# The up projection of a squared-ReLU MLP as seven products of halves, with its weights streaming

## The reference, cut to what matters

```python
h = rmsnorm(x, mix_norm)
b_gate, c_gate, v = jnp.split(h @ w_in, 3, axis=-1)      # (512 x 2048) @ (2048 x 6144)
y = (b_gate * causal_conv3(c_gate * v)) @ w_out          # (512 x 2048) @ (2048 x 2048)
x = x + y
g = rmsnorm(x, mlp_norm)
a = relu(g @ mlp_w1)                                     # (512 x 2048) @ (2048 x 8192)
x = x + (a * a) @ mlp_w2                                 # (512 x 8192) @ (8192 x 2048)
```

## Time and profile before

| | us |
|---|---|
| median of 3 runs (2037.37 to 2037.85) | 2037.64 |
| the profiled execution, whole | 2034.88 |
| its span, first to last instruction | 2033.1 |
| TensorE busy in it | 2015.3 (99%) |
| VectorE busy in it | 1217.7 (60%) |
| ScalarE busy in it | 657.8 (32%) |

### The profile page before, as it was taken

The page is one execution under the profiler, slowest core; times in us unless marked ns, Lnnn a source line. Parts: engine busy times, 40 slices in busy tenths (PEclk is TensorE's granted clock), DMA queues, the critical chain, the costliest instruction groups (busy, mean ns, idle before and its releaser), DMA issues.

```text
span 2033.1 us, 22629 instructions
## 1 busy us (share of the span) xinstructions
PE 2015.3 (99%) x8900; PEld 1665.6 (82%) x8900; DVE 1217.7 (60%) x1362; ACT 657.8 (32%) x876; POOL 30.6 (2%) x62
## 2 busy tenths in 40 slices
PE   8999999999999999999999999999999999999999
PEld 7888888888888888787888888888888888888887
DVE  6345353353543453535364554636988989978878
ACT  6222222222233332323232232323444443333432
POOL 0000000000000000000000000000000000000000
PEclk9999999999999999999999999999999999999999
DMA  5322223222223222536263553639899888888783
GB/s 187 114 93 103 95 91 104 97 88 103 83 104 103 100 87 104 196 118 229 99 248 128 204 198 138 244 108 364 321 359 353 314 336 316 320 316 322 272 316 139
DMA packets 72965, 387.10 MB, mean 190 GB/s; under 512 B 7984, under 2 KB 7984, under 8 KB 41264
## 3 DMA queue, kind: packets, MB, share of 16 engines
q1 hardware_dynamic: 64672, 327.18, 44.3%
q0 software_dynamic: 8064, 58.72, 6.9%
q10 hardware_dynamic: 144, 0.04, 0.0%
HBM read 323.00 MB, written 62.91 MB: 190 GB/s over the span
## 4 chain that ended last, share of the span: by engine, by line
PE 99%; issue 0%; DMA 0%; ACT 0%; DVE 0%; ACTq 0%
PE pair L682 68%; PE pair L781 30%; PE pair L748 0%; DMA cols<-in_cols 0%; PE pair L712 0%; PE pair L705 0%; PE pair L715 0%; PE pair L718 0%; ACT L284 0%; DVE x L601 0%; ACT h_hi L284 0%; ACT w_hi L280 0%; ACTq L340 0%
## 5 line engine op out<-in xcount | busy, mean ns | idle before, releaser
L391 DVE TENSOR_TENSOR w_lo<-w_raw,w_hi 128x512 fp32r<-128x512 f32 x512 | 352.3, 692 | 677.2 <-ACT w_hi L280 671.9
L682 PE MATMUL pair<-h_hi,w_lo 128*128 128x512 f32 x1788 | 698.5, 391 | 6.9 <-issue 6.9
L682 PE MATMUL pair<-h_hi,w_hi 128*128 128x512 f32 x1788 | 695.9, 389 | 0.0
L682 PE MATMUL pair<-h_lo,w_hi 128*128 128x512 f32 x1788 | 695.6, 389 | 0.0
L280 ACT ACTIVATE w_hi<-w_raw 128x512 fp32r<-128x512 f32 x512 | 323.0, 631 | 951.6 <-PE pair L682 949.1
L781 PE MATMUL pair<-d_w,act_hi 128*128 128x512 f32 x1792 | 551.6, 389 | 0.0
L682 PEld LDWEIGHTS pair<-h_hi,w_lo 128*128 128x128 f32 x1788 | 335.6, 188 | 78.2 <-issue 9.5
L781 PEld LDWEIGHTS pair<-d_w,act_hi 128*128 128x128 f32 x1792 | 336.3, 188 | 69.9 <-issue 0.2
L682 PEld LDWEIGHTS pair<-h_hi,w_hi 128*128 128x128 f32 x1788 | 335.6, 188 | 70.2
L682 PEld LDWEIGHTS pair<-h_lo,w_hi 128*128 128x128 f32 x1788 | 335.7, 188 | 69.7 <-issue 0.5
L333 ACT ACTIVATE d_w<-d_raw 128x1024 fp32r<-128x1024 f32 x224 | 233.7, 1059 | 369.6 <-PE pair L781 235.3
(11 more groups left out here) (55 smaller groups left out, 571.9 us busy)
## 6 DMA issues: line engine op xcount, KB each, us to landing
w_raw<-in_weights SPq DMA_DIRECT2D x127, 1024.0 KB, 4.9
d_raw<-in_down SPq DMA_DIRECT2D x64, 1024.0 KB, 8.5
spill<-stage POOLq DMA_DIRECT2D x56, 1024.0 KB, 6.0
act_hi<-spill SPq DMA_DIRECT2D x112, 512.0 KB, 6.5
act_lo<-spill SPq DMA_DIRECT2D x112, 512.0 KB, 7.3
resid<-in_xt SPq DMA_DIRECT2D x3, 1024.0 KB, 12.9
out<-x SPq DMA_DIRECT2D x6, 512.0 KB, 3.3
resid<-in_xt SPq DMA_DIRECT2D x4, 256.0 KB, 6.0
```

Source lines behind the costliest of these rows:

```text
L391: nc.vector.tensor_tensor(w_lo[:, k % RING, :], w_raw[:, k // GRAN % NRAW, k % GRAN, :], w_hi[:, k % RING, :].bitcast(F32), ALU.subtract). ...
L682: mm = nc.tensor.matmul(ps[NT * parity + i], stationary, moving, start=(k == 0 and j == 0), stop=(k == KT - 1 and j == 2))
```

## The change

The up projection is done in the same seven-product way. The 16 up blocks go; 16 more turns stand ahead of the 16 of the down projection, numbered `v` = 0 to 15 (`UP` = 16, `NV` = 32), with the same slots, ring and T1 to T4. A pair of turns, even and odd, makes 1024 features of the MLP for all tokens, the even turn from one half of the model width and the odd from the other. Activations are stationary now, so the result has tokens on partitions. ScalarE copies an even turn's five rotating products and the sum L11 to SBUF (`copy_product`, `copy_first`), and VectorE joins them with the odd turn's by 12 additions of 128x1024 a pair (`add_up`). The four quadrants are scaled and rectified by ScalarE (`rectify`, eight operations of 128x512 a pair), turned over by TensorE (`turn_quad`, four groups of eight transposes a pair, in slots 0, 2, 3 and 4 of the next even turn) and squared by ScalarE out of PSUM (`square_quad`, four of 128x1024 a pair).

The four combinations and seven splits of a pair's result (`form_z`, `split_z_hi`, `split_z_lo`) then run in the following two turns, at the slots in `SPLIT_AT` and `FORM_AT`; the last pair's run in the down turns (`LATE`). Staging is three buffers of 4 KB a partition, and high and low part of an item go out as two DMAs of 512 KB. The high part of item n takes buffer 2n mod 3 and the low part the next one, each when the DMA that last used the buffer has landed.

The activations of the up turns are seven combinations for the even turns and seven for the odd; four of each stay in SBUF, and three (`SHARED`) are kept in HBM and loaded anew every turn from `v` = 2 on, 1 MB each. They are made during the output blocks and turn 0. The output blocks come in the order 0, 2, 1, 3; the residual is turned over behind each of them and goes to HBM (`mixed`), to be loaded in turn 15. Each output block from the third on waits for the residual group of two blocks before (`turn_taken`). The square sums of the second norm are now turned into 1/rms on 128x4 values in turn 1.

The core of the diff (removed lines are left out, but for one):

```diff
-TURN_AT = (5, 8, 11, 14)
+TURN_AT = (8, 10, 12, 14)
+OUT_ORDER = (0, 2, 1, 3)
...
+ROTATE = (S1, S2, S3, S4, L22)
+SHARED = (S2, S4, L22)
...
+FIRST_SPLIT = {(1, 11): 0, (1, 12): 1, (1, 13): 2, (1, 15): 3, (2, 0): 4, (2, 2): 5, (2, 4): 6}
+FIRST_FORM = {(1, 14): (0, 1), (2, 1): (2,), (2, 3): (3,)}
+SECOND = (L11, L12, S1, S3, S2, S4, L22)
+SECOND_SPLIT = {(0, 6): 0, (0, 7): 1, (0, 9): 2, (0, 10): 3, (0, 11): 4, (1, 1): 5, (1, 3): 6}
+SECOND_FORM = {(0, 8): (0, 1), (0, 10): (2,), (0, 12): (3,)}
+SPLIT_AT = {(0, 5): 0, (0, 8): 1, (0, 9): 2, (0, 11): 3, (0, 13): 4, (1, 1): 5, (1, 3): 6}
+FORM_AT = {(0, 10): (0, 1), (0, 12): (2,), (1, 2): (3,)}
+LATE = {(0, 9): 0, (1, 5): 1, (1, 12): 2, (2, 12): 3, (3, 5): 4, (3, 12): 5, (4, 12): 6}
+LATE_FORM = {(2, 5): (0, 1), (3, 9): (2,), (4, 5): (3,)}
...
+        stage = [at("stage0", RESID + 24 * KB, [P, NT, HALF], F32R), at("stage1", RESID + 28 * KB, [P, NT, HALF], F32R),
+                 at("stage2", TMP, [P, NT, HALF], F32R)]
...
+        def read_out(eng, n):
+            v, i = n // 5, n % 5
+            if v >= UP:
+                eng.wait_ge(taken, n - 5 * UP + 1)
+            elif v % 2:
+                eng.wait_ge(added, 12 * (v // 2) + (2, 3, 8, 11, 12)[i])
+            else:
+                eng.wait_ge(copied, 5 * (v // 2) + i + 1)
...
+                sp.wait_ge(w_used, KT * (NB - 1) + GRAN * (r + 1))
+                load_raw(0, r)
+            for v in range(NV - 1):
+                after = v + 1
+                down = after >= UP
+                if after == 2:
+                    sp.wait_ge(act_out, 16 * 2 * 2 * len(SHARED))
+                if down:
+                    spills_done(sp, (after - UP) % NC)
+                if after == UP:
+                    sp.wait_ge(turn_out, 16 * KT)
                 for j, r in enumerate((None, R11, R12, R22, R21, None, None)):
+                    if down:
+                        if after == UP and j not in SHARED:
+                            product_done(sp, v - 1, j)
+                        else:
+                            product_done(sp, v, j)
+                        load_act(spill[(after - UP) % NC], j)
+                    elif after > 1 and j in SHARED:
+                        product_done(sp, v, j)
+                        load_act(act_kept[after % 2], j)
                     if r == R11:
+                        sp.wait_ge(t_formed, 4 * v + T4)
+                        load_raw(after, r)
                     elif r is not None:
+                        sp.wait_ge(lo_ready, SLOTS * v + {R12: 10, R22: 12, R21: 14}[r])
+                        load_raw(after, r)
+                    if after == UP and j in (L11, S1, L12, S3):
+                        product_done(sp, v, j)
+                        q, place = {L11: ("11", x11), S1: ("21", x21), L12: ("22", x22), S3: ("12", x12)}[j]
+                        load_mixed(q, place)
...
+            def put_spill(c, n):
+                for half in range(2):
+                    w = 2 * (NPROD * c + n) + half
+                    pool.wait_ge((stage_hi, stage_lo)[half], NPROD * c + n + 1)
+                    pool.dma_start(spill[c, SPILLS[n], half], stage[w % 3][:].bitcast(F32)).then_inc(spilled[w % 3], 16)
...
+            def rectify(q, m):
+                o, t = ((q_first, 0), (q_s1, 1), (q_s4, 0), (q_l22, 1))[m]
+                act.wait_ge(added, 12 * q + (6, 9, 11, 12)[m])
+                if q == 0 and m == 0:
+                    act.wait_ge(norm_step, 4)
+                for i in range(2):
+                    nc.scalar.activation(o[:, i, :], o[:, i, :], ACT.Relu,
+                                         scale=rstd_t[:, 2 * t + i:2 * t + i + 1]).then_inc(rectified, 1)
+            def square_quad(q, m):
+                act.wait_ge(quad_turned, 4 * q + m + 1)
+                if q > 0:
+                    act.wait_ge(stage_lo, NPROD * q)
+                nc.scalar.activation(quad[("L11", "L22", "L12", "L21")[m]].rearrange("p a t -> p (a t)"),
+                                     pairs[1][:].rearrange("p a t -> p (a t)"), ACT.Square).then_inc(quad_ready, 1)
+            def split_z_hi(c, n):
+                w = 2 * (NPROD * c + n)
+                act.wait_ge(quad_ready, 4 * c + {0: 1, 1: 3, 2: 2}.get(n, 4))
+                if n in FORMED:
+                    act.wait_ge(z_formed, 4 * c + FORMED[n])
+                if w >= 3:
+                    act.wait_ge(spilled[w % 3], 16 * (w // 3))
+                nc.scalar.activation(stage[w % 3][:], quad[HOLDS[SPILLS[n]]], ACT.Copy).then_inc(stage_hi, 1)
...
+                    if v < UP and v % 2 == 0:
+                        if s in (7, 9, 13):
+                            copy_product(v, {7: 0, 9: 1, 13: 2}[s])
+                    if v < UP and v % 2 == 1:
+                        if s in (1, 3):
+                            copy_product(v - 1, {1: 3, 3: 4}[s])
+                        if s == 5:
+                            copy_first(q)
+                        if s == 13:
+                            rectify(q, 0)
+                    if 2 <= v <= UP and v % 2 == 0:
+                        if s in (2, 3, 4):
+                            rectify(q - 1, s - 1)
+                        if s in (3, 5, 6, 7):
+                            square_quad(q - 1, {3: 0, 5: 1, 6: 2, 7: 3}[s])
+                    if 2 <= v < UP and (v % 2, s) in SPLIT_AT:
+                        split_z_hi(q - 1, SPLIT_AT[v % 2, s])
...
+            def split_z_lo(c, n):
+                w = 2 * (NPROD * c + n)
+                dve.wait_ge(stage_hi, NPROD * c + n + 1)
+                if w + 1 >= 3:
+                    dve.wait_ge(spilled[(w + 1) % 3], 16 * ((w + 1) // 3))
+                    dve.wait_ge(stage_lo, NPROD * c + n)
+                nc.vector.tensor_tensor(stage[(w + 1) % 3][:], quad[HOLDS[SPILLS[n]]], stage[w % 3][:].bitcast(F32),
+                                        ALU.subtract).then_inc(stage_lo, 1)
...
+            def add_up(q, n):
+                v = 2 * q + 1
+                done = 12 * q
+                bank = {2: S1, 3: S2, 6: L12, 8: S3, 11: S4, 12: L22}.get(n)
+                if bank == L12:
+                    other = pairs[1][:]
+                elif bank is not None:
+                    other = pairs[2 + (5 * v + ROTATE.index(bank)) % 2][:]
+                else:
+                    other = {1: q_first, 4: q_s1, 5: q_s2, 7: q_s2, 9: q_s3, 10: q_s3}[n][:]
+                o = (q_s2, q_s1, q_s2, q_s4, q_s3, q_first, q_s4, q_s3, q_s1, q_l22, q_s4, q_l22)[n - 1][:]
+                if bank is not None:
+                    product_done(dve, v, bank)
+                if n == 1:
+                    dve.wait_ge(first_copied, q + 1)
+                if n in (1, 2, 4, 5, 10):
+                    dve.wait_ge(copied, 5 * q + {1: 2, 2: 1, 4: 4, 5: 3, 10: 5}[n])
+                if n > 2:
+                    dve.wait_ge(added, done + {3: 1, 4: 2, 5: 3, 6: 1, 7: 4, 8: 5, 9: 8, 10: 8, 11: 7, 12: 10}[n])
+                nc.vector.tensor_tensor(o, other, o, ALU.add).then_inc(added, 1)
...
+                    if 0 < v <= UP and v % 2 == 0:
+                        if s == 0:
+                            add_up(q - 1, 9)
+                            add_up(q - 1, 10)
+                        if s == 1:
+                            add_up(q - 1, 11)
+                        if s == 3:
+                            add_up(q - 1, 12)
...
+                    if v < UP and v % 2:
+                        if s == 6:
+                            add_up(q, 1)
+                        if s == 7:
+                            add_up(q, 2)
+                        if s == 9:
+                            add_up(q, 3)
+                        if s == 10:
+                            add_up(q, 4)
+                            add_up(q, 5)
+                        if s == 11:
+                            add_up(q, 6)
+                        if s == 12:
+                            add_up(q, 7)
+                        if s == 13:
+                            add_up(q, 8)
+                    if 2 <= v < UP and (v % 2, s) in SPLIT_AT:
+                        split_z_lo(q - 1, SPLIT_AT[v % 2, s])
+                    if 2 <= v < UP:
+                        for f in FORM_AT.get((v % 2, s), ()):
+                            form_z(q - 1, f)
...
+            def turn_quad(q, m):
+                o = (q_first, q_s1, q_s4, q_l22)[m]
+                pe.wait_ge(rectified, 8 * q + 2 * m + 2)
+                if m > 0:
+                    pe.wait_ge(quad_ready, 4 * q + m)
+                view = pairs[1][:].rearrange("p a (b t) -> p (a b) t", b=2)
+                for i in range(NT):
+                    for t in range(2):
+                        tr = nc.tensor.transpose(view[:, i, P * t:P * (t + 1)], o[:, t, P * i:P * (i + 1)], eye[:])
+                tr.then_inc(quad_turned, 1)
...
+            def banks_of_product(v, j):
+                u = v - UP
+                if j in ROTATE:
```

(41 more changed lines are left out.)

639 lines of the change are left out of this document (382 added, 257 removed).

## The result

The changed kernel takes 2051.76 us in the median of four runs (2047.96 to 2054.16), the kernel before 2037.51 on the same chip (2035.11 to 2037.85, four runs). The ratio is 1.0071, with a 95% interval of 1.0053 to 1.0088: slower by 0.7%. The forecast was 1980.0, with 2003 as its upper end. Of the profiled execution's own time, 2047.96 us, the forecast's sum had 1977.1: 70.9 us are to be found.

The account below looks back on a forecast made before the run. TensorE, busy in 99% of the span, was taken as the bound: 2034.88 - 87.1 + 25.7 - 3.45 = 1970.0 us, plus waits of 3.5, 2.6 and 1.0 = 1977.1. With 2.8 to the median, 1980; range 1972 to 2003.

Parts of the forecast that it names:

- TensorE's account: Up projection: 3072 matmuls become 2688, saving 87.1 us; new transposes cost 25.7; two holes fewer, -3.45; 1970.0 us without waits.
- Pair 0: First two up turns, fuller than the others: TensorE waits 0.6, 0.6 and 1.4 us, 2.6 in all.
- Turn 15's crowd of loads: SyncE's queue must bring weights, activations and residual within 38 us, at 395 GB/s; 1 us taken.
- VectorE's account: VectorE's work in a pair of up turns: 75.6 us overlapped, about 77.5 with waits, against TensorE's 79.4.
- The rival in which VectorE is the bound: VectorE operations in up turns run end to end: 2.2 us a pair, 1994 us, up to 2000; chance 0.2.
- "no cost" of the staging buffers: `split_z_lo` waiting for the previous item's high-part DMA costs nothing; upper end 3.0 us a pair, 21 us.
- L - 5.6: Cost in us a pair of a staging write landing in L us, at item 2, the closest case.
- Staging writes land late: Rival: up-turn staging writes landing at 8.6 us give 2001, at 15.3 us 2048; chance 0.14.
- VectorE has done each one slot or more before TensorE comes to it: The chain from `add_up` 9 to 12 through rectification, transpose and square, costed at nothing.
- It fits with 0.3 us to spare.: Odd turn, before slot 12: VectorE's run up to `add_up` 8 takes 37.8 us within 14 slots, 38.08 us.
- the transposes: 32 new groups of eight on TensorE, 0.80 us each, 25.7 us in all; 28.2 by another figure.
- Stalls: TensorE's waits in pairs 1 to 7: 0.5 us each, 3.5 in all; 1.5 each if VectorE operations ran end to end.

Follow-up runs that it names:

- the best version: Changed kernel with seven staging places, squares in earlier slots, T2 ahead of `add_up` 12, S3 read out earlier, items 5 and 6 later: 1979.82 us, ratio 0.9721.
- The places alone: Changed kernel with seven staging places in place of three, nothing else: 2037.96 us.
- the later items: Changed kernel with only item 5 moved to slot 3, item 6 to slot 6 and form 3 to slot 1 of the odd turn: 2035.1 us.
- the version with places and later items: Changed kernel with seven staging places and items 5 and 6 later; squares, T2 and S3's read-out unchanged: 2013.8 us.
- The order in all: Changed kernel with squares in slots 2, 3, 5 and 6, T2 ahead of `add_up` 12 and S3 read out earlier; three staging places: 2024.2 us.
- the squares alone: Changed kernel with only ScalarE's four squares of a pair moved from slots 3, 5, 6, 7 to 2, 3, 5, 6: 2035.08 us.
- the three versions with places and order: Changed kernel with seven staging places and earlier squares, then T2 ahead of `add_up` 12 as well, then S3 read out earlier too: 2014.12, 2008.66 and 2007.93 us.

## Why the prediction was wrong

TensorE's account is there and its size is right. What failed is what the prediction put at nothing: the landings of the spills and the late squares.

**Held.** 5376 matmuls behind the output blocks and 256 transposes; the down turns in one piece; holes of 2.5 us in all at the output blocks, where four had made 6.9 and 3.45 were to remain. Pair 0: TensorE waited 0.78 and 0.57 us in turn 0 and 0.74 ahead of turn 1's slot 12, 2.1 in all where 2.6 were taken. Turn 15's crowd of loads cost nothing (its pair in the best version takes 80.0). VectorE's account of 75.6 to 77.5 us a pair measured 76.8 of busy time. The rival in which VectorE is the bound fails: with the order and places mended, operations follow each other after 1.13 us all through the dense run, and the pair is TensorE's. The best version's VectorE:

```profile
1220.66 1.22 DVE L815 TENSOR_TENSOR ring<-raw,ring 128x1024 fp32r<-128x1024 f32 x1
1221.79 1.22 DVE L757 TENSOR_TENSOR q_first_r<-quads,stage 128x1024 fp32r<-128x1024 f32 x1
1222.93 1.22 DVE L815 TENSOR_TENSOR ring<-raw,ring 128x1024 fp32r<-128x1024 f32 x1
1224.06 1.22 DVE L757 TENSOR_TENSOR q_l_r<-quads,q_s_r 128x1024 fp32r<-128x1024 f32 x1
```

The Trainium skill (VectorE: DVE Perf Modes, The DRAIN you can't avoid) has the next operation start when the pipe is empty, and adds that one that is not held starts earlier. These rows, like the earlier trace rows, show the earlier start.

**Failed: "no cost" of the staging buffers.** The step took a landing of 3.3 to 4.3 us from the earlier trace rows and one place, item 2, with "L - 5.6". The landing was 6.9 in the median, and 7.3 to 8.1 at this one place, by which that formula gives 1.7 to 2.5 us a pair; VectorE waited 7.3 (51.3 / 7) and ScalarE 5.0 (35.2 / 7). So both the landing and the count of places were wrong. The argument against late landings was a mean, 265 GB/s (measured: 248), where the stretch that held the landings carried 345 to 390. And with three buffers in rotation every item from 2 on waits for a landing, on both engines. VectorE's wait at item 2 itself, 4.6 to 5.4 us, is what the step's own figures give for such landings (L - 2.6, before the idle time behind it is taken off); item 5 then waited again, on VectorE and, in every pair, on ScalarE, whose wait the step left out, and for that it made no sum. The places alone gave 14 us, the later items 17, both 38. The rival "Staging writes land late" was thus right in its mechanism, and it put the point at which it decides at 14 us of landing, where 7 to 8 at item 2 and 6 to 11 at item 5 were enough. The Trainium skill (DMA: Bandwidth & Descriptors, Anatomy of one DMA) gave 3.2 us by an estimate. In the best version the same 512 KB from the same queue landed in 2.9 us for the last low part of a pair and in 12.6 at `q_l_r`: by the windows the DMA engines moved 172 GB/s in all during one of the first (1255.0 to 1258.5 us), little more than this write itself, and 400 GB/s during one of the second (1225.3 to 1237.9). So the trace agrees with the figure where hardly anything else is moved, and not elsewhere.

**Failed: "VectorE has done each one slot or more before TensorE comes to it"**, of the chain from `add_up` 9 to 12 through rectification, transposes and squares. VectorE had, but the squares are ScalarE's, and ScalarE's program puts the second behind high parts that wait for T2. The wait was summed on the engine that has the work, not on the one whose order holds it up. Price: 3.1 us a pair, and 1.6 of clock in six of seven pairs of the version with places and later items; in the changed kernel the clock fell behind this hole in three of eight places. The order in all gave 28 us when alone, the squares alone 17.

**Failed: "It fits with 0.3 us to spare."** The 37.8 us assume that VectorE comes to the run without delay. With 7 us of VectorE's waits on spills in each pair, the run of 14 slots is late, slot 12's gate is late by up to 1.3 in every odd turn (9.8 us in 8), and no slack is there to win anything back. The sum itself held: in the version with places and later items, which reads S3 out where the changed kernel does, this gate was late once, by 0.8 us. That the edits are worth more together (72) than the sum of the parts (58) may come from this; no run shows it.

**Mis-sized: the transposes**, 0.80 us a group. In the best version a group and 12 matmuls take 3.63 us from start to start (1204.81 to 1208.44 us), less 2.72 is 0.91, above both values weighed (0.80 and 0.88); 32 x 0.11 = 3.5 us in all.

**Slips in its sums**, none of which changes this account. With 0.3 us to issue, 2.9 and 2.7 us of cover give L - 5.3 and not L - 5.6. Stalls of up to 12 us on 1973 end at 1985 and not 1987. The 265 and 395 GB/s count a MB as 2^20 bytes and are held against the 345 of the view, which counts 10^6: in its unit they are 277 and 413. VectorE operations that run end to end cost 1.5 us a pair under "Stalls" and 2.2 in the rival.

The sum itself came out: a pair is 28 x 2.72 + 4 x 0.91 = 79.8 us, and the version without waits takes 80.4 in the mean and 1979.8 us in the whole, where the forecast was 1980. That the two agree so closely is in part luck: the seven pairs took 6.8 us over 555.8 where 3.5 were allowed, turn 15 nothing where 1.0 was, the two holes 2.5 where 3.45 were left. Of the 69.6 us by which its span is shorter than the changed kernel's (2046.2 less 1976.6), the seven pairs hold 63.3 (625.90 less 562.60), and the last pair's turn, 16, most of the rest. What stays open: how the extra 14 us of the combination divide. Whether loads spread evenly over the turn would bring three buffers to the same end was not tried.

## What to carry to other kernels

Take the load of the DMA engines in stretches of 10 us around the wait, not as a mean of a turn, and walk a rotation of few buffers through every use. For each result that another engine needs, go through the program of the engine that makes it, and ask what the instruction ahead of it waits for. A margin of 0.3 us is no margin while any wait lies ahead of it; count the waits first.

## What was not expected of the hardware

A quarter of the bytes did not land in a quarter of the time: 128 KB took 4.4 us in the median where 512 KB took 6.9, in the same places. A hole of 2.8 us in TensorE's work was followed by the lower clock (0.62 granted over 4.5 us; the 12 matmuls in 4.42 instead of 2.84 us) in the version with places and later items; in the changed kernel only some pairs show it (0.96 in the second, 1.00 in the sixth, at the same hole of 2.81 us). In the three versions with places and order, where TensorE's holes are up to 1.9 us long, the clock is 1.000, as it is in the best version, where none in the up turns is longer than 0.9.
